# Input projection of a two-layer hybrid backbone: the stored copy of x goes out in thirds, one modulation product moves into the first pair of groups, a weight split moves ahead of the norm's roots, and GpSimd's weight differences are cut into four operations

## The reference

```python
for each of 2 layers:
    sh1, sc1, ga1, sh2, sc2, ga2 = split(silu(c) @ w_mod + b_mod, 6)      # and the same for c_ctx
    h  = rms_norm(x,  g_norm1) * (1 + sc1)  + sh1
    hc = rms_norm(xc, g_norm1) * (1 + sc1c) + sh1c
    z, zc = h @ w_in, hc @ w_in                # four head groups: global GQA, window GQA, GLA, mLSTM
    o_a, o_b = attention with rotary / window + sink
    o_c = bidirectional GLA scan (decays from z), gated norm
    o_d = bidirectional mLSTM scan (gates from z), gated norm
    x = x + ga1 * (concat(o_a, o_b, o_c, o_d) @ w_out)
    x = x + ga2 * (square(relu(h2 @ w_mlp1)) @ w_mlp2)    # h2: second norm, modulated
    (the same for xc in the first layer)
```

## Time and profile before

| | |
|---|---|
| three executions | 1944.5, 1947.41, 1947.5 us |
| profiled execution | 1946.74 us, span 1945.0 us |
| TensorE busy | 1779.0 us, 91% of the span |
| VectorE, ScalarE, GpSimd busy | 1110.4, 744.7, 383.6 us |
| mean granted TensorE clock | 0.956 of full speed |
| chain that ended last | TensorE 74%, VectorE 11%, issue 5%, DMA 4%, ScalarE 3%, GpSimd 2% |

### The profile page before, as it was taken

How to read it: one execution, slowest core, us unless ns; L and a number is a source line. 1 busy time by engine, 2 the same in 40 slices (tenths; PEclk the granted TensorE clock), 3 DMA queues, 4 the chain that set the end, 5 groups by cost and what they waited for, 6 DMA issues and landing times.

```text
span 1945.0 us, 27792 instructions
## 1 busy us (share of the span) xinstructions
PE 1779.0 (91%) x11328; PEld 1539.0 (79%) x11328; DVE 1110.4 (57%) x1638; ACT 744.7 (38%) x1026; POOL 383.6 (20%) x124
## 2 busy tenths in 40 slices
PE   6898999988897999999999968999988979999998
PEld 4687897767786989999899958888667768777776
DVE  3373746676646797797987946554666541212132
ACT  4432325643225634535435453333553252313130
POOL 0131632100210000000000023352100324433431
PEclk8899999998998999999999989999898989999999
DMA  8630112000055517547275132212200212232221
GB/s 322 205 139 23 54 56 92 40 1 1 1 195 194 217 68 299 208 166 301 78 276 216 43 117 88 86 66 77 87 2 1 87 65 87 86 108 86 87 87 65
DMA packets 33855, 217.61 MB, mean 112 GB/s; under 512 B 4660, under 2 KB 5082, under 8 KB 15322
## 3 DMA queue, kind: packets, MB, share of 16 engines
q1 hardware_dynamic: 33754, 216.19, 30.0%
HBM read 196.77 MB, written 19.40 MB: 111 GB/s over the span
## 4 chain that ended last, share of the span: by engine, by line
PE 74%; DVE 11%; issue 5%; DMA 4%; ACT 3%; POOL 2%; SPq 0%; DVEq 0%; ACTq 0%; POOLq 0%
PE ps L2335 25%; PE ps L2764 19%; PE ps L2507 9%; PE ps L2322 3%; PE ps L2589 2%; DMA raw<-w_modl 2%; DMA first_mod<-w_modl 1%; DVE xT L2067 1%; PE ps L2704 1%; POOL w_lo L696 1%; PE ps L2279 1%; PE ps L2440 1%; PE ps L2635 1%; DVE w_lo L2027 1%; PE ps L2642 1%
## 5 line engine op out<-in xcount | busy, mean ns | idle before, releaser
L696 POOL TENSOR_TENSOR w_lo<-raw,w_hi 128x2048 fp32r<-128x2048 f32 x64 | 296.7, 4637 | 1235.3 <-ACT w_hi L800 1235.3
L2764 PE MATMUL ps<-op_hi,w_hi 128*128 128x384 f32 x896 | 307.8, 343 | 22.1 <-DVE xT L2067 9.2
L2764 PE MATMUL ps<-op_lo,w_hi 128*128 128x384 f32 x896 | 305.0, 340 | 0.0
L2764 PE MATMUL ps<-op_hi,w_lo 128*128 128x384 f32 x896 | 304.5, 340 | 0.0
L800 ACT ACTIVATE w_hi<-raw 128x2048 fp32r<-128x2048 f32 x64 | 122.2, 1909 | 199.3 <-PE ps L2335 131.0
L2764 PEld LDWEIGHTS ps<-op_hi,w_hi 128*128 128x128 f32 x896 | 171.3, 191 | 29.7 <-issue 17.4
L2335 PE MATMUL ps<-h_hi,w_hi 128*128 128x512 f32 x496 | 168.1, 381 | 3.8 <-POOL w_lo L696 3.7
L2764 PEld LDWEIGHTS ps<-op_hi,w_lo 128*128 128x128 f32 x896 | 171.4, 191 | 0.0
L2764 PEld LDWEIGHTS ps<-op_lo,w_hi 128*128 128x128 f32 x896 | 171.2, 191 | 0.0
L2335 PE MATMUL ps<-h_lo,w_hi 128*128 128x512 f32 x496 | 163.4, 372 | 0.0
L2335 PE MATMUL ps<-h_hi,w_lo 128*128 128x512 f32 x496 | 162.8, 370 | 0.0
(11 more groups left out here) (333 smaller groups left out, 3627.9 us busy)
## 6 DMA issues: line engine op xcount, KB each, us to landing
raw<-w_big SPq DMA_DIRECT2D x96, 1024.0 KB, 4.8
raw_m<-w_modl SPq DMA_DIRECT2D x20, 1024.0 KB, 5.9
raw<-w_modl SPq DMA_DIRECT2D x16, 1024.0 KB, 5.0
op_hi<-op_cache SPq DMA_DIRECT2D x21, 768.0 KB, 4.7
op_lo<-op_cache SPq DMA_DIRECT2D x21, 768.0 KB, 6.2
first_mod<-w_modl SPq DMA_DIRECT2D x8, 1024.0 KB, 19.0
x_keep<-xT SPq DMA_DIRECT2D x2, 3072.0 KB, 14.2
xT<-x_keep SPq DMA_DIRECT2D x2, 3072.0 KB, 9.9
```

The lines of the kernel that those rows point to most:

```text
L696: nc.gpsimd.tensor_tensor(w_lo[r][:], raw[raw_r][:], w_hi[r][:].bitcast(F32), ALU.subtract).then_inc(sem("lo_ready"), 1)
L2764: ins = mm(bank(base + g, 0, h), wide(w)[:, k, g * P:(g + 1) * P], ops[hl][:, k, 0:h], start=(p in FRESH and k == 0 and q == 0), stop=(k = ...
```

## The change

Five edits:

- The store of `xT` goes out in three parts of 2, 3 and 3 feature blocks (768, 1152 and 1152 KB), one each behind the weight loads of slots 0, 1 and 2 of the projection's loop, in both layers. Who waits for `x_kept` now waits for all three.
- In the first layer the product of the modulation slice of (0, 1) moves from behind the first pair of groups into its middle, ahead of feature block 4, into another 256 columns of PSUM bank 7. VectorE's first copy waits for both products.
- The columns and the bias of a modulation slice are written in the code at the head of the next group instead of at the end of the own.
- In the second layer ScalarE's split of slot 1 moves from behind the norm's eight blocks to ahead of the second half's roots.
- GpSimd's weight difference is four operations over 128 x 512 elements instead of one over 128 x 2048. Only the last signals `lo_ready`.

```diff
+LOW_PARTS = 4
+KEEP_PARTS = 3
@@ SP, the loop over the projection's slots
                     if s == 0:
                         sp.wait_ge(sem("t_ready"), KD + 3 * KD * l)
-                        sp.dma_start(x_keep.rearrange("p (k t) -> p k t", k=KD), xT[:]).then_inc(sem("x_kept"), 16)
+                    if s < KEEP_PARTS:
+                        ks = slice(s * KD // KEEP_PARTS, (s + 1) * KD // KEEP_PARTS)
+                        sp.dma_start(x_keep.rearrange("p (k t) -> p k t", k=KD)[:, ks, :],
+                                     xT[:, ks, :]).then_inc(sem("x_kept"), 16)
@@ the three waits for x_kept (SP, ScalarE, VectorE)
-                sp.wait_ge(sem("x_kept"), 16 * (l + 1))
+                sp.wait_ge(sem("x_kept"), 16 * KEEP_PARTS * (l + 1))
@@ GpSimd
                 gp.wait_ge(sem("hi_ready"), n)
-                nc.gpsimd.tensor_tensor(w_lo[r][:], raw[raw_r][:], w_hi[r][:].bitcast(F32),
-                                        ALU.subtract).then_inc(sem("lo_ready"), 1)
+                for x in range(LOW_PARTS):
+                    ks = slice(x * KD // LOW_PARTS, (x + 1) * KD // LOW_PARTS)
+                    ins = nc.gpsimd.tensor_tensor(w_lo[r][:, ks, :], raw[raw_r][:, ks, :],
+                                                  w_hi[r][:, ks, :].bitcast(F32), ALU.subtract)
+                ins.then_inc(sem("lo_ready"), 1)
@@ ScalarE, norm
-                rstd(*((slice(0, HALF), bank(4, 0, HALF)) if l == 1 and which == 1 else (slice(0, n_t), bank(4, 0, n_t))))
+                if l == 1 and which == 1:
+                    split_hi(PROJ + 1)
+                    rstd(slice(0, HALF), bank(4, 0, HALF))
+                else:
+                    rstd(slice(0, n_t), bank(4, 0, n_t))
...
-                if which == 1:
-                    split_hi(l * PROJ + 1)
+                if l == 0 and which == 1:
+                    split_hi(1)
@@ VectorE, in_proj
+                        if pending is not None and (s, m) in GROUPS:
+                            mod_out(pending)
+                            pending = None
                         if in_mod(l, s, m) is not None:
-                            mod_copy()
+                            pending = in_mod(l, s, m)
+                            if s == 0:
+                                mod_copy(bank(7, 256 * (1 - m), WC), 2 - m)
+                            else:
+                                mod_copy()
...
-                        if in_mod(l, s, m) is not None:
-                            mod_out(in_mod(l, s, m))
@@ TensorE, feature_pair
                 for k in range(KD):
+                    if second_mod and k == KD // 2:
+                        pe.wait_ge(sem("mod_landed"), mods.at(2) * 16)
+                        mod_rows_of(7 * 512, raw[1]).then_inc(sem("mod_summed"), 1)
                     pe.wait_ge(ready[0], ready[1] + k + 1)
@@ TensorE, in_proj
-                        if has_mod:
+                        if pending:
+                            mod_columns()
+                        if has_mod and (s, m) != (0, 1):
                             mod_rows_sum()
+                        pending = has_mod
...
-                        if has_mod:
-                            mod_columns()
```

More of the change, by code:

```diff
@@ L932, in own_pairs @@
                     j0, nt = halves(l)[hf]
-                    act.wait_ge(sem("x_kept"), 16 * (l + 1))
+                    act.wait_ge(sem("x_kept"), 16 * KEEP_PARTS * (l + 1))
                     act.wait_ge(sem("lev_done"), 16 * l + hf + 1)
@@ L1407, in mod_out, with mod_copy @@
                                 bc(b, 2), ALU.add).then_inc(sem("mod_out"), 1)
-            def mod_copy(src=bank(7, 256, WC)):
-                dve.wait_ge(sem("mod_summed"), sum_n.at(1))
+            def mod_copy(src=bank(7, 256, WC), ahead=1):
+                dve.wait_ge(sem("mod_summed"), sum_n.at(ahead))
                 dve.wait_ge(sem("mod_used"), sum_n.at(FIRST_MODS))
@@ L1549, in gla_step @@
                     last.then_inc(sem("ex_raw"), 1)
-                    dve.wait_ge(sem("x_kept"), 16 * (l + 1))
+                    dve.wait_ge(sem("x_kept"), 16 * KEEP_PARTS * (l + 1))
                     v.memset(snap[:, 0, ORDER[0][0], :], 0.0)
@@ L2312, in passes, with feature_pair @@
                 return ((w_hi[r], 0), (w_hi[r], 1), (w_lo[r], 0))
-            def feature_pair(g, r, mov, n_ts, ready):
+            def feature_pair(g, r, mov, n_ts, ready, second_mod=False):
                 for k in range(KD):
+                    if second_mod and k == KD // 2:
+                        pe.wait_ge(sem("mod_landed"), mods.at(2) * 16)
+                        mod_rows_of(7 * 512, raw[1]).then_inc(sem("mod_summed"), 1)
                     pe.wait_ge(ready[0], ready[1] + k + 1)
@@ L2481, in in_proj @@
                 h0 = T_("h").n
+                pending = False
                 for s in range(IN_SLOTS):
@@ L2495, in in_proj @@
                         if (s, m) == (0, 0):
-                            feature_pair(0, r, (h_hi, h_lo), (n_q(l), T), (sem("h_ready"), h0))
+                            feature_pair(0, r, (h_hi, h_lo), (n_q(l), T), (sem("h_ready"), h0),
+                                         in_mod(l, 0, 1) is not None)
                         elif s == 0:
```

## The result

The changed kernel takes 1925.25 us (median of 6 runs, 1921.48 to 1930.06), the kernel before 1945.95 beside it (6 runs): 20.7 us less by the medians. The ratio is 0.991, which is 17.5 us, with a 95% interval of [0.9894, 0.9926], so 14.4 to 20.6 us; the difference of the medians lies at its edge. Forecast were 1931.0 us and 1922 to 1941. The profiled execution took 1930.06 us, the slowest of the six; its span is 1927.5 us against 1945.0. So the traces account for 17.5 us, and the terms are read against that. These are two single executions: the kernel before alone took 1935.0 to 1948.4 us in 25 executions on one chip, a spread larger than most terms.

The account below looks back on a forecast made before the run. TensorE was busy for 91% of the span, so only its idle and half-speed stretches could give time back. First layer 3.5 and second layer 12.2 us sum to 15.7 off 1946.74: 1931.0 us, range 1922 to 1941.

Parts of the forecast that it names:

- (a): First layer: slot 2's first group starts at 84.5 instead of 91.70, with half speed saved in it; 7.7 us gained.
- (b): First layer: VectorE waits for the store's last third, landing at 117.3; 2.2 us lost (0 to 3.5).
- (c): First layer's VectorE chain: two differences cost 5.0 each instead of 4.3; 1.4 us lost together (0 to 2.2).
- (d): First layer: GpSimd's exponents stand behind a difference, TensorE's level products wait for `sacc`; 0.6 us lost.
- (e): Second layer, slot 1's earlier split: waits of 3.7 and 3.0 and half speed go, norm 2.8 later; 7.0 us gained.
- (f): Second layer: the 5.3 us wait for `ex` shrinks, its multiplication behind one to three operations; +1.0 us (-0.5 to 3.0).
- (h): Second layer: the 2.3 us wait before L2478 goes, with about 1.4 us of half speed; +3.7 us (2.3 to 4).
- (g): Second layer: TensorE's wait of 3.2 us for `sacc` grows; 0.65 us lost.
- (i): Second layer's second norm: `h_lo` comes two operations earlier, TensorE starts 1.9 us earlier; +1.1 us (0 to 1.9).
- taken back: Rival: half speed in the first pair, dearer store and norm collision, no gain at `ex`; 1940.2 us, chance 0.17.
- Everything given: Rival: store lands in time, operations fit into the norm, `ex` behind one operation; 1923.1 us, chance 0.13.
- slower rival: Second layer's MLP loop: GpSimd's four operations cost far more than 1.28 us each; 1952 us, chance 0.05.

Follow-up runs that it names:

- late_split: Changed kernel with the split of the second layer's slot 1 behind the norm again: 1936.13 us, ratio 0.9967.
- changed_again: The changed kernel run once more, unaltered: 1925.3 us, ratio 0.9912.
- rest_at_slot_1: Changed kernel with the store in two parts, two feature blocks behind slot 2's load, six behind slot 3's: 1922.33 us, ratio 0.9884.
- whole_diff: Changed kernel with GpSimd's weight difference in one operation again: 1932.22 us, ratio 0.9948.
- product_behind_pair: Changed kernel with the product of modulation slice (0, 1) behind the first pair of groups again: 1927.81 us, ratio 0.9936.
- turn_early: As rest_at_slot_1, with VectorE's sum and copy for group (4, 0)'s turn moved ahead of the second half of the scans: 1914.73 us, ratio 0.985.
- two_parts: Changed kernel with the weight difference in two operations instead of four: 1922.78 us, ratio 0.9889.
- four_parts_only: Kernel before with only the weight difference split into four operations: 1938.2 us, ratio 0.9978.
- whole_store: Changed kernel with the whole store in one part behind slot 2's load again: 1929.26 us, ratio 0.9925.
- eight_parts: Changed kernel with the weight difference in eight operations instead of four: 1932.02 us, ratio 0.9929.
- turn_early_two_parts: turn_early with the weight difference in two operations instead of four: 1913.79 us, ratio 0.9851.

## Why the prediction was right

The direction, the range and the time in the profile hold (16.7 us gained by the executions' own times, against 15.7). Term by term it is right for partly other reasons, and that the sum came so close is in part luck.

(a) held up to slot 2 and was too large there. The pair ended at 71.6 (said: 71.7), group (1, 0) began at 74.1 (74.4), slot 2's first group at 85.8 (84.5), and 1.0 us more went to the slower clock behind two short waits, which I had not counted: 4.8 us for 7.7. The same first layer began slot 2 at 84.42 in late_split and at 86.95 in changed_again, so the size moves by some 2.5 us between executions, with the wait for slice (0, 1) and the clock behind it.

(b) was mis-sized: VectorE lost 4.5 us (4.2 to 4.7 in the seven traces with the store in thirds), not 2.2, and more than the bound of 3.5. There are two causes. The third was issued at 111.21 instead of 107.6: the load ahead of it came 4.8 us earlier than before (110.73 against 115.56) and not 7.7, as TensorE's lead had shrunk to 4.8 by the products that SyncE waits for. And the third took 11.1 us to land beside two slices and slot 4, not 9.7. The recorded sum also has two slips that nearly cancel: it puts the third at 107.6, ahead of the load at 107.9 that it stands behind, and it adds 2 us, for which no row is named, to a rate of 0.41 MB per us that holds them already (6.1 MB in 14.9 us). rest_at_slot_1 shows the price: with that wait gone its level products are 3 us ahead of late_split's, whose first layer differs only in how the store is cut.

(c) had the wrong sign. VectorE did not pay 5.0 for each difference in four but 2.9 for the first: it got 2.3 us of its own work done in the five us that they overlapped. For the second, with GpSimd's exponents behind it, it paid 4.7, against 5.1 before. From `snap` to the turn's copy it took 28.7 us against 30.6 before and 29.5 in whole_diff, so the term is 0.8 to 1.8 gained, not 1.4 lost. By the Trainium skill (SBUF — State Buffer, "A bandwidth-pool intuition that's wrong") whoever was locked out goes on about 115 ns behind the other's end, measured there on a DMA's descriptors; by my estimate from that figure a difference would have cost 0.35 us more. The trace shows no such handover: contested scans start 1.41 and 1.37 us apart, less than one GpSimd operation (5.05 / 4 = 1.26) and one scan (0.42) together. (d) 0.9 lost (0.6).

First layer by the trace of after: 4.8 - 4.5 + 1.8 - 0.9 = 1.2 us at the level products, against 3.5; late_split's trace has 4.4 there. Another 1.7 come by the end of that layer and are in no term. In its attention the lead rises to 6.1 us and falls again; 1.3 of it are 12 matmuls that took 1.53 us instead of 2.82 behind an equal wait, at a granted clock of 1.00 instead of 0.50. The rest is not taken apart.

(e) 8.0 against 7.0: roots 0.6 later as said, the third block 1.7 later against its roots, together 2.3 (said: 2.8). Both waits and their half speed went. (f) was the term that failed by most: +5.9 less 1.1 at `snap`, 4.8 against 1.0 (up to 3.0). The first multiplication was ready 2.0 us after its issue instead of 5.1, as the alternation with one or two operations gives; what I left out is that the wait of 5.3 us had half speed behind it, as those of (e) and (h) had (12 matmuls in 5.08, now in 3.05), and that this is worth 2.6 us. Its bounds don't follow from its own terms either: 4.3 less 1.25 to 3.75 less 0.5 is 0.05 to 2.55. (g) 0.4 lost (0.65). (h) 3.0 (3.7): a wait of 1.4 us stays. (i) nothing (1.1): TensorE waits 2.0 us less for the norm, but the product ahead of that wait took 2.1 us instead of 1.1 and the 48 matmuls behind it 14.1 instead of 13.1. Second layer, with 0.9 lost between the rotation matmul and the last MLP: 14.5 against 12.2.

So *taken back* had the store right, even too cheap, and in changed_again the half speed in the pair; the rest of it did not come. *Everything given* had `ex` and nothing of the store. The slower rival's place shows 5.05 us per slot in the MLP loop and no wait. Against the trace of after, (a) and (b) were 2.9 and 2.3 us too good, (c) and (f) 3.2 and 3.8 too bad. The first layer's sum was 2.3 us too large and the second's 2.3 too small, so the total was closer than its parts.

## What to carry to other kernels

Where a long operation on one engine holds up another, as GpSimd's difference did VectorE here, splitting it is worth it if the other engine feeds a stalled TensorE. It costs where TensorE, or anything queued behind it, waits for its end: split it, and start it earlier. After a wait has been shortened, ask what VectorE's queue had been holding in front of a result that was ready: a copy of 0.4 us moved ahead in it gave 7.6 us. Price a removed wait of TensorE together with the half speed that the rows show behind it, and do so in every term: here it was counted in (e) and (h) and left out of (f).

## What the hardware showed that I had not expected

GpSimd's difference of 128 x 2048 alone takes 4.6, 4.77, 5.05 and 5.61 us in one, two, four and eight operations: about 0.15 us for each further one. Beside the four a scan of 0.42 us takes 1.36, less than 0.42 and 1.26 together, and the two memsets at 122.38 and 122.65 took their usual 0.27 us in the middle of them.

Executions of the same code differ by more than most terms. Slice (0, 1) was waited for 0.6, 1.4 and 2.7 us in three traces of the same first layer (after, late_split, changed_again). And 12 matmuls near 440 us in the first layer's attention, behind the same wait of 1.04 us, took 1.53 us in some traces (after, changed_again, product_behind_pair, rest_at_slot_1, turn_early, two_parts) and 2.82 in others (before, four_parts_only, whole_diff, late_split, whole_store, eight_parts, turn_early_two_parts); after and late_split have the same code up to there. With what lies around them that is 2 to 3 us. The granted clock was 1.00 and 0.50 (after and before). What decides is open, and a single profile of a kernel is uncertain by as much.
